# A fused two-block model kernel: the mixer's gated-state projections as three products of rounded high and low parts

## What is computed

```python
q_l, v_l = hgrn2_qv(lat)                      # silu(p[2]), p[5]
kf_l, gf_l = hgrn2_gates(lat[3], lb_fwd)      # f = lb + (1 - lb) * sigmoid(z); keys 1 - f, log f
kb_l, gb_l = hgrn2_gates(lat[4], lb_bwd)
# the same for the context; then, forwards and backwards, in chunks:
o_inter = jnp.einsum('bhtk,bhkv->bhtv', qc * jnp.exp(cum), state)
att = jnp.einsum('bhtk,bhtsk,bhsk->bhts', qc, decay, kc)
state = jnp.exp(last)[..., None] * state + einsum(kc * exp(last - cum), vc)
y_hg_lat = hgrn2_readout(o_lf + flip(o_lb), lat[6], hg_norm_g)
y = g_mla * y_mla + g_hg * y_hg               # merge_branches, g = sigmoid(p[7]), sigmoid(p[8])
```

## Time and profile before

| | us |
|---|---|
| median of 3 runs (3814.2 to 3822.3) | 3819.18 |
| profiled execution | 3820.7 |
| its span | 3818.8 |

### The profile page before, as it was taken

How to read it: one execution, slowest core, us unless ns; L and a number is a source line. 1 busy time by engine, 2 the same in 40 slices (tenths; PEclk the granted TensorE clock), 3 DMA queues, 4 the chain that set the end, 5 groups by cost and what they waited for, 6 DMA issues and landing times.

```text
span 3818.8 us, 55172 instructions
## 1 busy us (share of the span) xinstructions
PE 3659.6 (96%) x23376; PEld 2597.9 (68%) x23376; DVE 1880.7 (49%) x3411; ACT 1123.2 (29%) x1721; POOL 319.3 (8%) x205
## 2 busy tenths in 40 slices
PE   8999999999999999999999999999899999999997
PEld 7789988888887899888888865767643333332333
DVE  4485666768655855677686434455521111111111
ACT  3223244444533232444445312333210000000011
POOL 0013300000000133000000000112100000000000
PEclk9899999999998999999999999999899999999999
DMA  5534444445445444444455322211389999999996
GB/s 198 213 141 166 140 159 164 169 176 188 166 166 195 151 167 140 148 173 177 177 177 190 129 81 100 74 50 75 130 370 422 427 428 427 427 428 427 427 427 273
DMA packets 81022, 846.21 MB, mean 222 GB/s; under 512 B 8896, under 2 KB 11072, under 8 KB 12512
## 3 DMA queue, kind: packets, MB, share of 16 engines
q1 hardware_dynamic: 80768, 842.60, 56.3%
HBM read 841.52 MB, written 1.05 MB: 221 GB/s over the span
## 4 chain that ended last, share of the span: by engine, by line
PE 79%; DMA 11%; DVE 7%; ACT 2%; issue 1%; POOL 0%; DVEq 0%; ACTq 0%; SPq 0%
PE bank L87 77%; DMA ring<-in_w_gu_dram 11%; DVE arena L123 2%; ACT arena L113 1%; PE bank L100 1%; DVE arena L191 1%; DVE arena L137 1%; DVE arena L185 1%; DVE arena L167 0%; DVE arena L155 0%; DVE arena L197 0%; DVE arena L131 0%; DVE ring_rounded L123 0%; DMA ring<-in_w_inA_dram 0%; DVE arena L129 0%
## 5 line engine op out<-in xcount | busy, mean ns | idle before, releaser
L87 PE MATMUL bank<-arena 128*128 128x32 f16 (+7 forms) x8020 | 922.8, 328 | 41.6 <-DVE arena L123 17.3
L87 PEld LDWEIGHTS bank<-arena 128*128 128x128 f16 (+4 forms) x8020 | 503.0, 132 | 456.2 <-issue 338.3
L113 ACT ACTIVATE arena<-bank 128x256 f32<-128x256 f32 (+2 forms) x443 | 203.0, 458 | 1229.7 <-PE bank L87 1008.4
L123 DVE TENSOR_TENSOR arena<-arena 128x512 f16<-128x512 f16 (+6 forms) x768 | 514.7, 696 | 55.1 <-ACT arena L113 40.0
L87 PE MATMUL bank<-ring,arena 128*64 128x512 f32 (+1 forms) x1968 | 502.8, 595 | 40.6 <-DMA ring<-in_w_gu_dram 36.7
L87 PE MATMUL bank<-xT,ring 128*128 128x256 f32 (+1 forms) x2208 | 458.4, 365 | 14.3 <-DMA ring<-in_w_inA_dram 11.3
L87 PE MATMUL bank<-xhi,uhi 128*128 128x256 f32 x1552 | 453.9, 292 | 15.2 <-DVE arena L129 8.7
L87 PE MATMUL bank<-xlo,uhi 128*128 128x256 f32 x1552 | 437.8, 282 | 0.0
L87 PE MATMUL bank<-xhi,ring_rounded 128*128 128x256 f32 x1552 | 435.6, 281 | 0.0
L87 PEld LDWEIGHTS bank<-xT,ring 128*128 128x128 f32 x2208 | 388.3, 192 | 61.4 <-issue 11.9
L87 PEld LDWEIGHTS bank<-ring,arena 128*64 128x64 f32 (+1 forms) x1968 | 170.6, 144 | 361.5 <-issue 284.2
(11 more groups left out here) (137 smaller groups left out, 2952.3 us busy)
## 6 DMA issues: line engine op xcount, KB each, us to landing
ring<-in_w_gu_dram SPq DMA_DIRECT2D x97, 2048.0 KB, 22.8
ring<-in_peer_u_dram SPq DMA_DIRECT2D x128, 1024.0 KB, 6.6
ring<-in_peer_v_dram SPq DMA_DIRECT2D x128, 1024.0 KB, 5.2
arena<-in_w_dn_dram SPq DMA_DIRECT2D x62, 2048.0 KB, 21.1
arena<-in_w_gu_dram SPq DMA_DIRECT2D x43, 2048.0 KB, 21.0
ring<-in_w_hg_dram SPq DMA_DIRECT2D x14, 2048.0 KB, 8.7
ring<-in_w_mod_dram SPq DMA_DIRECT2D x12, 2048.0 KB, 8.2
ring<-in_w_inA_dram SPq DMA_DIRECT2D x8, 2048.0 KB, 8.2
```

The source lines that it names most:

```text
L87: i = self.e.matmul(o, l, r, start=start, stop=stop)
L113: self.e.activation(o, i, f, scale=scale, **kw).then_inc(self.sem, 1)
L123: self.e.tensor_tensor(o, a, b, op).then_inc(self.sem, 1)
```

## The change

All 48 tasks are formed as three products on rounded (float32r) data: high part of the weights by high part of `h`, high by low, low by high. So a task has 24 products in place of 8. The parts are made like this:

- `h`: ScalarE rounds two halves of 2048 elements (`act_h_high`), one behind the gates of attention, one behind the third step of the softmax; VectorE subtracts (`dve_h_split`), one behind the first rotation, one behind the copy of the seventh turned softmax block. The high parts stand in the old `uhi` tile and in half of one ring place (`parts_at`), which is held until the last readout; two places are left for the matrices.
- weights: per task, ScalarE rounds 1024 elements (`act_high`) into one of two places in the other half of that ring place; GpSimd subtracts (`pool_low`) in place, over the matrix in the ring. The first two tasks are rounded at the end of attention; every other one, `i + 2`, inside `act_task` of task `i`, behind its copy.
- a value task is now a quarter of the width for all four groups of tokens, into four banks taken together; they are copied out behind the fourth. The one task in the readout of unit 1 is now the first query of the second half, not its first value.
- in units 1 and 3 GpSimd does the subtractions for all tasks of `before_keys[u]` ahead of the differences of levels 0 and 1; in units 0 and 2 those for the queries.

```diff
-        before_keys = {0: q_tasks(0) + v_tasks(0), 1: gate_tasks(0), 2: q_tasks(1) + v_tasks(1)[1:], 3: gate_tasks(1)[:6]}
+        before_keys = {0: q_tasks(0) + v_tasks(0), 1: gate_tasks(0), 2: q_tasks(1)[1:] + v_tasks(1), 3: gate_tasks(1)[:6]}
-        in_readout = {0: v_tasks(1)[0:1], 1: []}
+        in_readout = {0: q_tasks(1)[0:1], 1: []}
...
         def pe_task(kind, k, ct):
-            P.wait_ge(*at["landed", ("w_hg", kind, k)])
-            w = ring.of("w_hg", kind, k)[:, 0:PIECE].rearrange("p (c n) -> p c n", c=8)
-            cs = slice(ct * 128, ct * 128 + 128)
-            b, (s, n) = banks.take(kind, k, ct)
-            P.wait_ge(s, n)
+            P.wait_ge(*at["hg split", kind, k, ct])
+            for i in range(2):
+                P.wait_ge(*at["h split", i])
+            hi, lo = task_high(kind, k, ct), task_low(kind, k, ct)
             if kind == "v":
-                P.mm(b[:, :], [(hT[:, dc, cs], w[:, dc, :]) for dc in range(8)])
+                for t in range(4):
...
+                    for c in range(2):
+                        dc = 2 * ct + c
+                        for i, (h, w) in enumerate(((h_high(dc), hi), (h_lo[:, dc, :], hi), (h_high(dc), lo))):
...
-                P.mm(b[:, 0:cols], [(w[:, dc, cs], hT[:, dc, 0:cols]) for dc in range(8)])
+                b, (s, n) = banks.take(kind, k, ct)
+                P.wait_ge(s, n)
+                P.mm(b[:, 0:cols], [(w[:, dc, :], h) for dc in range(8) for w, h in
+                                    ((hi, h_high(dc)[:, 0:cols]), (hi, h_lo[:, dc, 0:cols]), (lo, h_high(dc)[:, 0:cols]))])
...
+        def act_high(i):
+            if i < len(in_turn):
+                kind, k, ct = in_turn[i]
+                A.wait_ge(*at["landed", ("w_hg", kind, k)])
+                if i >= 2:
+                    A.wait_ge(*at["hg", *in_turn[i - 2]])
+                A.act(task_high(kind, k, ct), task_of(kind, k, ct), ACT.Copy)
+                A.mark("hg high", kind, k, ct)
+
+        def pool_low(i):
...
+                G.wait_ge(*at["hg high", kind, k, ct])
+                G.tt(task_low(kind, k, ct), task_of(kind, k, ct), task_high(kind, k, ct).bitcast(F32), SUB, lag=FREE)
+                G.mark("hg split", kind, k, ct)
...
+        def dve_h_split(i):
...
+            V.wait_ge(*at["h high", i])
+            V.wait_ge(*at["proj", 3, "w_gm", 1])
+            V.tt(h_lo[:, 4 * i:4 * i + 4, :], hT[:, 4 * i:4 * i + 4, :], src.bitcast(F32), SUB, lag=FREE)
...
         def act_task(kind, k, ct):
+            A.wait_ge(*at["hg", kind, k, ct])
+            if kind != "v":
+                act_evict(kind, k, ct)
+            elif ct == 3:
+                for t in range(4):
+                    act_evict(kind, k, t)
+            act_high(number[kind, k, ct] + 2)
...
+            p = parts_at()
+            ring.tenant[2 * p] = ring.tenant[2 * p + 1] = ("hg parts",)
+            ring.in_turn([ring.place["w_qb_r",] // 2, ring.place["w_hg", "f", 0] // 2])
...
+            ring.back(P, "hg parts")
...
+            for i in range(2):
+                act_high(i)
             end_stage_name(A, "A")
...
-                    for task in before_keys[u][:4]:
+                    for task in before_keys[u][:4 - hh]:
                         act_task(*task)
                     A.act(qh, qh, ACT.Silu)
...
             for u, (hh, r) in enumerate(units):
+                first, rest = (before_keys[u][:4 - hh], before_keys[u][4 - hh:]) if r == 0 else (before_keys[u], [])
...
+                for task in first:
+                    pool_low(number[task] + 2)
+                pool_level(u, 0)
+                pool_level(u, 1)
+                for task in rest:
+                    pool_low(number[task] + 2)
                 for lv in range(7):
-                    pool_level(u, lv)
+                    if lv < 5:
+                        pool_level(u, lv + 2)
+                    if lv % 2 == 0 and lv // 2 < len(in_levels[u]):
+                        pool_low(number[in_levels[u][lv // 2]] + 2)
```

More of the change, by code:

```diff
@@ L316, in build @@
         with nc.sbuf_tensor("arena", [128, ARENA], F32) as arena:
+            pass
+        with nc.sbuf_tensor("h_rounded", [128, 2048 + PIECE], F32R) as h_r:
             pass
@@ L1582, in build @@
         ym = ar3(8, 256)
+        hT_at = top[0]
         hT = ar3(8, 512)
@@ L1629, in build @@
         mixer_end = max(mixer_end, top[0])
+        assert mixer_end <= ARENA - SPLIT + 4608
+        mixer_end = ARENA - SPLIT + 4608 + 2048
+        h_hi = uhi_t[:, :].rearrange("p (c t) -> p c t", c=4)
+        h_lo = h_r[:, hT_at:hT_at + PIECE].rearrange("p (c t) -> p c t", c=8)
         units = [(0, 0), (0, 1), (1, 0), (1, 1)]
@@ L1647, in gate_tasks, with parts_at, h_high, task_cols @@
             return [("ga", hh, ct) for ct in range(4)] + [("gb", hh, ct) for ct in range(4)]
-        before_keys = {0: q_tasks(0) + v_tasks(0), 1: gate_tasks(0), 2: q_tasks(1) + v_tasks(1)[1:], 3: gate_tasks(1)[:6]}
+        before_keys = {0: q_tasks(0) + v_tasks(0), 1: gate_tasks(0), 2: q_tasks(1)[1:] + v_tasks(1), 3: gate_tasks(1)[:6]}
         in_levels = {0: f_tasks(1), 1: f_tasks(2), 2: f_tasks(3), 3: gate_tasks(1)[6:]}
-        in_readout = {0: v_tasks(1)[0:1], 1: []}
+        in_readout = {0: q_tasks(1)[0:1], 1: []}
+        in_turn = f_tasks(0)
+        for u_, (hh_, r_) in enumerate(units):
+            in_turn = in_turn + before_keys[u_] + in_levels[u_] + (in_readout[hh_] if r_ else [])
+        number = {task: i for i, task in enumerate(in_turn)}
+        def parts_at():
+            return ring.place.get(("w_qb_n", 1), 0) // 2
+        def h_high(dc):
+            if dc < 4:
+                return h_hi[:, dc, :]
+            i = parts_at() * PIECE + (dc - 4) * 512
+            return ringr_t[:, i:i + 512]
+        def task_cols(block, kind, ct):
+            w = block.rearrange("p (c n) -> p c n", c=8)
+            return w[:, 2 * ct:2 * ct + 2, :] if kind == "v" else w[:, :, ct * 128:ct * 128 + 128]
+        def task_of(kind, k, ct):
+            return task_cols(ring.of("w_hg", kind, k)[:, 0:PIECE], kind, ct)
+        def task_low(kind, k, ct):
+            i = ring.place.get(("w_hg", kind, k), 0) * HALF
+            return task_cols(ringr_t[:, i:i + PIECE], kind, ct)
+        def task_high(kind, k, ct):
+            i = parts_at() * PIECE + HALF + number[kind, k, ct] % 2 * 1024
+            return ringr_t[:, i:i + 1024].rearrange("p (c n) -> p c n", c=2 if kind == "v" else 8)
         def task_src(kind, k):
@@ L2160, in dve_mixer @@
             dve_rope(0)
+            dve_h_split(0)
             V.wait_ge(*at["q rope in"])
@@ L2185, in dve_mixer @@
                 banks.back(V, "pT", i)
+                if i == 6:
+                    dve_h_split(1)
             dve_av(7)
@@ L2329, in act_mixer @@
                     act_rms(x_rstd, 512, 256, "kv")
+            act_h_high(0)
             for h in range(8):
@@ L2344, in act_mixer @@
                 act_exp_p(i + 2)
+                if i == 2:
+                    act_h_high(1)
+            for i in range(2):
+                act_high(i)
             end_stage_name(A, "A")
@@ L2371, in act_mixer @@
                     act_level(u, 1)
-                    for task in before_keys[u][4:]:
+                    for task in before_keys[u][4 - hh:]:
                         act_task(*task)
@@ L2423, in pool_mixer @@
             end_stage_name(G, "G")
+            for i in range(2):
+                pool_low(i)
             after_attention(G)
+            for task in f_tasks(0):
+                pool_low(number[task] + 2)
             for u, (hh, r) in enumerate(units):
+                first, rest = (before_keys[u][:4 - hh], before_keys[u][4 - hh:]) if r == 0 else (before_keys[u], [])
                 if u:
@@ L2430, in pool_mixer @@
                 G.mark("att cleared", u)
-                for lv in range(7):
-                    pool_level(u, lv)
+                for task in first:
[3 more added lines that the diff above has]
+                for task in rest:
+                    pool_low(number[task] + 2)
+                for lv in range(7):
+                    if lv < 5:
+                        pool_level(u, lv + 2)
+                    if lv % 2 == 0 and lv // 2 < len(in_levels[u]):
+                        pool_low(number[in_levels[u][lv // 2]] + 2)
+                if r:
+                    for task in in_readout[hh]:
+                        pool_low(number[task] + 2)
             end_stage(G, "G", "mixer")
@@ L2506, in sp_moe @@
         def sp_moe():
-            r = [(ring.n // 2 + i) % NSLOT for i in range(NSLOT)]
+            r = [parts_at()] + [ring.place["w_o2", j] // 2 for j in range(2)]
             ring.in_turn([NSLOT, r[0], NSLOT + 1, NSLOT + 2, r[1], r[2]])
```

19 lines of the change are left out of this document (18 added, 1 removed).

## The result

The changed kernel takes **3929.69 us** (median, 3928.95 to 3931.79) against 3819.12 before, ratio 1.0292, 95% interval 1.0274 to 1.0309: 110 us slower, 12 more than forecast. Its profiled execution spans 3927.9 us, 109.1 more than before.

A forecast was written before the change was run, and what follows sets the result against it. TensorE sets the pace in the mixer's stretch, beside a serial ScalarE and VectorE chain per unit. 99.9 - 5.3 + 1.1 - 3 - 0.6 + 1 + 3 + 2.3 = +98 us: 3918 us, range 3882 to 3950.

The forecast's parts named there:

- the units: Units 0 to 3 of the mixer, from ScalarE's start to TensorE's state products: together +99.9 us.
- the start: Ahead of unit 0: first four forgets gain 5.3 us, one more rounding costs 1.1, the input's split 2.3.
- the levels: From state products to the next unit, units 0 to 2: wide tasks gain 5.3 us each, 1 kept, -3 in all.
- what stands behind unit 3's state products: Unit 3's remaining stretch after its state products: a gain of 0.6 us.
- part 3: Rounding queued behind each unit's chain on ScalarE, TensorE stands after two tasks: +18.7, +27.8, +29.3, +24.1 us.
- The clock: After each stand of TensorE, granted clock well under 1; first narrow task at 1.2 GHz takes 5.1 us.
- The 1.5 us that I gave the states for the clock: State products of units 0 and 1 follow a wait and run slower: 1.5 us each, 3 together.
- the readout: Behind unit 1: narrow task replacing a wide one is hidden by VectorE's readout; the additional rounding ahead costs 1 us.
- the rival in which VectorE and GpSimd block each other: In the levels, each of 12 subtractions holds one VectorE step for 2.4 us: +29, 3947 us; chance 6%.
- a hold between VectorE and GpSimd: Where both engines work together, the trace was read as agreeing with a hold of about 1 us at most.
- The rival in which the roundings run ahead: ScalarE and GpSimd ready the parts in time, some 35 of 47 us gained: 3784 us; chance 4%.
- U: Time from ScalarE's start of a unit to TensorE's start of its state products; forecast about 64, 60, 61 and 53 us.

The follow-up runs named there:

- e1: Changed kernel with the weights' rounding and subtraction left out beyond the first two tasks; total unreadable (other experts picked), ruler stretch 352.7 us against 482.7.
- e8: Changed kernel with four places for high parts instead of two, weights split four tasks ahead: 3885.8 us, ratio 1.0172.
- e2: Changed kernel with ScalarE's task work (copying out, rounding) moved up into the gaps of each unit's chain: 3899.5 us, ratio 1.0212.
- e3: Changed kernel with GpSimd's differences of levels 0 and 1 put ahead of all its subtractions of a unit: 3914.4 us, ratio 1.0246.
- e11: Changed kernel with GpSimd's four subtractions in a unit's levels moved two levels on: 3907.6 us, ratio 1.0226.
- e5: Changed kernel with GpSimd's first two subtractions held back until VectorE's last normalization of attention's rows is done: 3923.9 us, ratio 1.0281.
- e10: Kernel before with only the forget projections as three products, unit 2's two roundings placed behind the copies of the keys: 3804.9 us, ratio 0.9965.

## Why the prediction was right, and where it was not

The time (3918 forecast, 3929.7 measured) lay in the stated range, and the mechanism is shown, not only argued: e1 takes the parts away and all is gained back, and e8, e2 and e3 each shorten the stand or the wait that they name. The sum was 98 and the span grew by 109: the units took 3 less than forecast, the start 2 more, the levels 6 more, what stands behind unit 3's state products 2 more, and 3 lie outside the ruler.

- **The order on ScalarE (part 3)** was right in each unit: +17.7, +26.5, +29.9 and +22.5 us against +18.7, +27.8, +29.3 and +24.1, together 96.6 against 99.9. The stand is of 17.7 to 27.2 us, released by GpSimd. That of unit 2 is the longest: it begins at 2598.6, when the two tasks with parts are done and VectorE still reads unit 1 out.
- Inside the units part of this agreement is luck. The third task began 22.2 to 23.5 us behind ScalarE's start, and not 25.4, since the exponential ended at 19.1 (17.7 in unit 2) and not at 21.2: the differences no longer ran beside VectorE's subtractions (e3). I had taken the chain's length over unchanged. Behind the third task the units took 0.3 to 1.0 us more than forecast, unit 2 3.8 more.
- **The clock** fell as the prediction had it: 0.52 to 0.79 of full in the windows with a stand, 1.00 from 2400 to 2420, where TensorE was busy. The first narrow task and the second took 7.7 us from 2384.64, so the first some 4.9, near the 5.1 forecast for the lower of its two levels, 1.2 GHz. The 1.5 us that I gave the states for the clock came in unit 1 (the 40 products took 6.75 us) and not in unit 0 (4.70). Windows of after, columns as in the earlier trace rows:

```profile
2400.00:2420.00 20.00, 17.55 (x86) 14.37 (x85) 2.15 (x2) 6.57 (x8) 9.61 (x5) 1.00 0.06 12
2480.00:2500.00 20.00, 3.86 (x18) 3.86 (x19) 14.84 (x20) 7.05 (x9) 6.06 (x2) 0.52 0.00 0
...
2600.00:2620.00 20.00, 0.00 (x0) 0.00 (x0) 15.16 (x23) 7.81 (x7) 0.95 (x1) 0.59 0.00 0
```

- **The levels were mis-sized.** With the readout and the clock I counted a loss of 1 us over three units (-3 + 1 + 3); measured is a loss of 1.3, 5.4 and 0.7. The gain on TensorE was there, 5 us a unit (e1). But e11 shows 17.6 us lost to the place of the subtractions, where I had allowed 12.9 (3 us kept of a gain of 15.9). I had priced a wait of 1 to 2 us for two levels of a unit and left out what a wait sets off: 1.8 us of VectorE's time held in each unit, and slow products behind it. So the rival in which VectorE and GpSimd block each other is true in part. The stretch with the readout still has 4.3 us in e11 over e1: about 2 are the slow state products behind the wait of 9.2 us (6.75 for 4.70; forecast 1.5), about 2 a longer wait of TensorE for VectorE in the readout (5.19 us for 3.16; forecast 1). Behind unit 3's state products I forecast a gain of 0.6, and 1.6 were lost.
- **The start was mis-sized** by 2.3 us: -1.9 forecast (-5.3 + 1.1 + 2.3), +0.4 measured. I took GpSimd's first subtractions to lie beside idle engines; they held VectorE for 2.2 us. Without that (e5) the lead is 2.6 us below before.
- **A reading was wrong:** from the earlier trace rows I took a hold between VectorE and GpSimd to be 1 us at most. That row shows only what GpSimd loses. The kernel before already had VectorE held for 2.2 us in each chain (e3).
- **The rest:** 109.1 us of span are 1.4 ahead of the ruler, 106.0 on it and 1.8 behind it. The last stage wanders between 1114 and 1120 us over the kernels (e1 apart), so the 1.8 are not explained, and need not be.
- The rival in which the roundings run ahead (3784) would not have been reached even then: e1's ruler puts it at 3795, since the chain bounds U at 29 to 32 us.

## What to carry to other kernels

A saving on the engine that sets the pace counts only where that engine is what comes last; ahead of a serial chain it buys nothing, and the preparation that it needs can undo the overlap. Ask of each prepared operand how many are in hand when the engine that prepares them goes away, what is queued behind the preparing instruction, and which engine it holds up while it runs. And divide a change by place: the third of its tasks that lay on the path was worth 14 us with the parts made at idle moments (e10), and the whole of it cost 110.

## What the runs showed of the hardware

VectorE and GpSimd held each other, at the most for nearly the whole of an instruction: 0.49 became 2.66 us for a scaling beside a subtraction of 2.3, two multiplications went from 1.42 to 3.49 us, eight scans beside two subtractions from 5.77 to 9.77, and a pair of subtractions from 4.65 to 6.09. The prediction had counted a hold of 1 us at most. The Trainium skill, SBUF — State Buffer, section "SBUF: two separate sides", has the later of two such instructions wait for the whole of the earlier, where VectorE's is in its two-port mode or, against one of GpSimd that reads SBUF, has two inputs in SBUF. These rows agree with it: the 2.17 us added to the scaling are nearly one subtraction. Not every meeting costs that; in e11 two multiplications beside the differences and a subtraction took 1.71.
